# Spreading expert gates with two float32r products instead of one fp32 product, and dealing the routing calls one per chunk

## The reference

```python
def peer(hn, w_q, subkeys, u, v):          # 8 heads, 16 experts per head
    q = (xt @ w_q).reshape(T, H, 2, PEER_QDIM // 2)
    s = jnp.einsum('thcd,cnd->thcn', q, subkeys)
    s1, i1 = lax.top_k(s[:, :, 0], K)
    s2, i2 = lax.top_k(s[:, :, 1], K)
    cand = (s1[..., :, None] + s2[..., None, :]).reshape(T, H, K * K)
    sc, ci = lax.top_k(cand, K)
    e1 = jnp.take_along_axis(i1, ci // K, axis=-1)
    e2 = jnp.take_along_axis(i2, ci % K, axis=-1)
    g = jax.nn.softmax(sc, axis=-1)
    # per token: sum over its 128 chosen experts of gelu(x . u[idx]) * g * v[idx], idx = e1 * 128 + e2
```

## Time and profile before

| | |
|---|---|
| median of 3 runs | 4156.8 us (4156.66 to 4158.11) |
| profiled execution | 4158.48 us, of which span 4157.2 us |
| PE busy / weight loads busy | 3895.5 us (94%) / 3108.8 us (75%) |
| DVE / ACT / POOL busy | 2220.1 (53%) / 1493.4 (36%) / 493.3 us (12%) |
| mean granted TensorE clock | 0.97 of 2.4 GHz |
| chain that ended last | PE 78%, DVE 10%, ACT 5%, DMA 3%, issue 2%, POOL 1% |

### The profile page before, as it was taken

One profiled execution on the slowest core, in us unless ns is written; L12 is line 12 of the kernel. 1 busy time (PEld: TensorE's weight loads), 2 busy tenths in 40 slices (PEclk: granted clock), 3 DMA queues, 4 the chain that ended last, 5 costly groups with the idle time before them and its releaser, 6 DMA issues.

```text
span 4157.2 us, 48351 instructions
## 1 busy us (share of the span) xinstructions
PE 3895.5 (94%) x19998; PEld 3108.8 (75%) x19998; DVE 2220.1 (53%) x3875; ACT 1493.4 (36%) x1876; POOL 493.3 (12%) x748
## 2 busy tenths in 40 slices
PE   6998989999899889988899989999998999999999
PEld 4755778888775568876777878878876788888887
DVE  2275553333557454455554355778873666654444
ACT  3245532122334633234554432435443322222222
POOL 0000000000000000000001000457655111100000
PEclk8999989999999999998999999999999999999999
DMA  5400113323120022231214233355455566543332
GB/s 191 150 34 1 61 41 122 122 102 122 61 76 8 21 71 91 102 128 49 77 41 138 74 116 121 133 162 164 161 172 180 185 186 191 182 149 112 114 127 83
DMA packets 109836, 459.81 MB, mean 111 GB/s; under 512 B 9216, under 2 KB 43120, under 8 KB 68912
## 3 DMA queue, kind: packets, MB, share of 16 engines
q1 hardware_dynamic: 82048, 354.96, 24.5%
q0 software_dynamic: 27568, 101.74, 8.2%
HBM read 389.04 MB, written 67.63 MB: 110 GB/s over the span
## 4 chain that ended last, share of the span: by engine, by line
PE 78%; DVE 10%; ACT 5%; DMA 3%; issue 2%; POOL 1%; SPq 0%; DVEq 0%; ACTq 0%; POOLq 0%
PE ps L566 21%; PE ps L567 21%; PE ps L568 21%; PE ps L2533 1%; PE ps L1176 1%; DMA gdram<-GST 1%; DVE ACC L1377 1%; DVE WL L451 1%; PE ps L480 1%; PE ps L645 1%; POOL Y L2669 1%; DVE MX L1350 1%; PE ps L1255 1%; ACT WH L440 1%; PE ps L2080 1%
## 5 line engine op out<-in xcount | busy, mean ns | idle before, releaser
L566 PE MATMUL ps<-HH,WH 128*128 128x512 f32 x2760 | 1060.0, 384 | 49.6 <-DVE HL L848 20.7
L567 PE MATMUL ps<-HL,WH 128*128 128x512 f32 x2760 | 1046.6, 379 | 0.0
L568 PE MATMUL ps<-HH,WL 128*128 128x512 f32 x2760 | 1042.7, 378 | 0.0
L451 DVE TENSOR_TENSOR WL<-stage,WH 128x2048 fp32r<-128x2048 f32 x248 | 567.4, 2288 | 449.6 <-ACT WH L440 449.6
L440 ACT ACTIVATE WH<-stage 128x2048 fp32r<-128x2048 f32 x248 | 472.7, 1906 | 564.1 <-PE ps L568 522.8
L566 PEld LDWEIGHTS ps<-HH,WH 128*128 128x128 f32 x2760 | 525.8, 191 | 160.2 <-issue 47.2
L568 PEld LDWEIGHTS ps<-HH,WL 128*128 128x128 f32 x2760 | 524.4, 190 | 104.8
L567 PEld LDWEIGHTS ps<-HL,WH 128*128 128x128 f32 x2760 | 525.9, 191 | 99.3 <-issue 1.2
L566 PE MATMUL ps<-AHp,WH 128*128 128x512 f32 x1024 | 404.4, 395 | 7.9 <-ACT Y L2851 7.9
L568 PE MATMUL ps<-AHp,WL 128*128 128x512 f32 x1024 | 404.2, 395 | 0.0
L567 PE MATMUL ps<-ALp,WH 128*128 128x512 f32 x1024 | 404.2, 395 | 0.0
(11 more groups left out here) (410 smaller groups left out, 4890.4 us busy)
## 6 DMA issues: line engine op xcount, KB each, us to landing
stage<-in_w SPq DMA_DIRECT2D x64, 1024.0 KB, 4.9
stage<-in_u SPq DMA_DIRECT2D x64, 1024.0 KB, 4.8
stage<-in_v SPq DMA_DIRECT2D x64, 1024.0 KB, 4.9
stage<-in_w_mod SPq DMA_DIRECT2D x48, 1024.0 KB, 4.9
GR<-gdram POOLq DMA_DIRECT2D x32, 1024.0 KB, 8.1
adram<-GR SPq DMA_DIRECT2D x22, 1024.0 KB, 3.9
AR<-adram POOLq DMA_DIRECT2D x88, 256.0 KB, 3.5
gdram<-GST SPq DMA_DIRECT2D x16, 1024.0 KB, 5.7
```

The lines of the kernel that those rows point to most:

```text
L451: dve.e.tensor_tensor(k.WL[o % 2][:, 0:w], k.stage[n % 2][:, 0:w], k.WH[o % 2][:, 0:w].bitcast(F32), ALU.subtract).then_inc(*dve.done("sla ...
L566: pe.e.matmul(o, wh[:, kk, cs], L.hh[:, kk, z], start=first, stop=False)
L567: pe.e.matmul(o, wh[:, kk, cs], L.hl[:, kk, z], start=False, stop=False)
L568: mm = pe.e.matmul(o, wl[:, kk, cs], L.hh[:, kk, z], start=False, stop=last)
```

## The change

1. The one-hot row with the gate is no longer one fp32 row. ACT copies the gates rounded to float32r (`GH`), DVE takes the remainder from PSUM (`GL`, piece "gates_lo", once per tile). The one-hot matrices become float32r.
2. DVE makes the one-hot rows of 8 tokens in one tensor_tensor of 128x1024 (`hot1`), and the rows times the remainder in a second one ("gated_lo"), where it had 8 tensor_scalar of 128x128. The rows times the rounded gate are made by ACT in place, 8 activations of 128x128 with a scale operand ("gated_hi"), one call after DVE's.
3. PE runs two float32r products per token with the same stationary operand, 16 in a batch, where it ran one fp32 product, 8 in a batch.
4. `route_order` deals the 23 choose pieces of a tile out over 14 calls for the first tile and over the 17 spread calls for the others, and one call follows each chunk: 14 + 4 x 17 = 82 calls for 84 chunks, so none is left over.
5. The waits for the route and the last stores move from before group 21 to its third chunk, just ahead of the weighing of group 0.
6. During the first product with `v`, ACT and DVE weigh group 1 at chunks 3 to 7 instead of 0 to 4 (`weighed_at`).

```diff
 def route_order():
-    phases = [[("choose", 0, 23)]] + [[("spread", t, 17), ("choose", t + 1, 23)] for t in range(3)] + [[("spread", 3, 17)]]
-    for phase in phases:
-        for i in range(max(n for _, _, n in phase)):
-            yield [(kind, tt, i) for kind, tt, n in phase if i < n]
+    for t in range(-1, 4):
+        calls = 14 if t < 0 else 17
+        for i in range(calls):
+            pieces = [("spread", t, i)] if t >= 0 else []
+            yield pieces + [("choose", t + 1, j) for j in range(23 * i // calls, 23 * (i + 1) // calls) if t < 3]
...
 # tensor_route
-                pe.wait_ge("hot1", (tt, b))
+                pe.wait_ge("gated_hi", (tt, b))
                 pe.wait_ge("hot2", (tt, b))
                 for t in range(8):
-                    mm = pe.e.matmul(p[:, 128 * t:128 * t + 128], oh[:, 1, t, :], oh[:, 0, t, :], start=True, stop=True)
+                    pe.e.matmul(p[:, 128 * t:128 * t + 128], oh[2][:, t, :], oh[0][:, t, :], start=True, stop=False)
+                    mm = pe.e.matmul(p[:, 128 * t:128 * t + 128], oh[2][:, t, :], oh[1][:, t, :], start=False, stop=True)
...
 # scalar_route
+        if kind == "spread" and i >= 1:
+            hi = k.OH.of((tt, i - 1))[0]
+            act.wait_ge("gated_lo", (tt, i - 1))
+            for t in range(8):
+                tok = 128 * tt + 8 * (i - 1) + t
+                op = act.e.activation(hi[:, t, :], hi[:, t, :].bitcast(F32), ACT.Copy, scale=k.GH[:, tok:tok + 1])
+            op.then_inc(*act.done("gated_hi", (tt, i - 1)))
...
 # vector_route
-            for t in range(8):
-                tok = 128 * tt + 8 * i + t
-                op = dve.e.tensor_scalar(oh[:, 0, t, :], k.IO[:, :], k.E1[:, tok:tok + 1], k.GG[:, tok:tok + 1],
-                                         ALU.is_equal, ALU.mult)
+            dve.e.tensor_tensor(oh[0], every_expert(k), every_token(k.E1[:, toks]), ALU.is_equal).then_inc(
+                *dve.done("hot1", (tt, i)))
+            dve.wait_ge("hot1", (tt, i))
+            dve.e.tensor_tensor(oh[1], oh[0].bitcast(F32), every_token(k.GL[:, toks]), ALU.mult).then_inc(
+                *dve.done("gated_lo", (tt, i)))
...
 # vector_early (scalar_early the same)
-            for _ in range(route_calls(c)):
-                vector_route(k, dve, next(route, []))
-    for pieces in route:
-        vector_route(k, dve, pieces)
+            vector_route(k, dve, next(route, []))
     dve.mark("route")
-    dve.wait_end("route", "pe", "act", "pool")
-    dve.wait_ge("gst_a", (3, 3))
-    dve.wait_ge("gst_b", (3, 3))
     for c in vector_linear(k, dve, u_linear(k, NPRE - 1)):
         if c == 2:
+            dve.wait_end("route", "pe", "act", "pool")
+            dve.wait_ge("gst_a", (3, 3))
+            dve.wait_ge("gst_b", (3, 3))
             for m in range(5):
                 vector_spilled(k, dve, 0, m)
...
+def weighed_at(g, c):
+    return c - 3 if g == 0 else c
...
             if g + 1 < NPRE:
-                vector_spilled(k, dve, g + 1, c)
+                vector_spilled(k, dve, g + 1, weighed_at(g, c))
```

More of the change, by code:

```diff
@@ L2775, in sync_early @@
                 sp.e.dma_start(io["adram"][g], k.GA.of(g).rearrange("p c t -> p (c t)")).then_inc(*sp.landed("aw", g))
-            for _ in range(route_calls(c)):
-                sync_route(k, sp, io, next(route, []))
-        if g == NPRE - 2:
-            for pieces in route:
-                sync_route(k, sp, io, pieces)
+            sync_route(k, sp, io, next(route, []))
 def p_linear(k, g):
```

56 lines of the change are left out of this document (30 added, 26 removed).

## The result

| | before | after |
|---|---|---|
| median | 4156.7 us | 4178.3 us |
| ratio | | 1.0054 (95% interval 1.0042 to 1.0066) |
| profiled execution / its span | 4158.5 / 4157.2 us | 4177.4 / 4176.1 us |
| first u matmul to first v matmul | 2530.04 to 3202.63, 672.6 us | 2526.81 to 3221.25, 694.4 us |
| POOL / ACT / DVE busy | 493 / 1493 / 2220 us | 620 / 1640 / 2227 us |

The change makes the kernel 21.5 us slower, where 4152 us was forecast. All of it is in the stretch of the route: 21.8 us more there; the profiled execution is only 18.9 longer, because this one came to the stretch 3.2 us earlier. Lines have moved: L566 to L568 are now L569 to L571, the spread product L2533 is L2546 and L2547, POOL's one-hot row L2669 is L2695, DVE's L2587 is the pair L2610 and L2614, ACT's new products are L2576, its copy L2563 is L2584.

The account below looks back on a forecast made before the run. PE was taken as the bound, losing 61.1 us (51.1 in the route, 10.0 at v). 4158.5 - 61.1 + 56.1 of new stops = 4153.5, and 4152 us as median; range 4138 to 4240.

Parts of the forecast that it names:

- Part 1: Spread batches on PE: 16 float32r products last 1.71 us as before, set by weight loads; worth 0.
- rival B: PE's spread products: 128-column float32r costs what fp32 does per column, batch 3.41 us; 4235 us, chance 0.25.
- rival D: PE's weight load is shorter than its pace shows (81 ns), saving 26 us on PE; 4146 us, chance 0.05.
- Part 2: Helpers per call: DVE unchanged, ACT 2.4 us more, POOL from 4.7 to some 6 us, held up by DVE's pair.
- The bookkeeping: Five queues followed call by call through the route; gave the new stops, and 46.5 us for the old order's 51.1.
- rival C: Helpers become the bound, by ACT's products at 0.39 us each or a longer DVE pair; 4170 us, chance 0.15.
- Part 3: New stops in the route: first tile 9.3, three spread tiles 37.1, last tile 5.1, plus 4.6; 56.1 us.
- Part 4: End of route and first product with v: the moved waits leave neither the 25.6 nor the 10.0 us.
- the 25.6: Loss from the bare calls to the first v matmul in the kernel before, in us; was to go.
- the 10.0: Loss in the first product with v in the kernel before, in us; was to go with later weighing.
- my own case: Whole kernel: batches stay 1.71 us and old stops give way to new ones; 4152 us, 4139 to 4167, chance 0.55.
- the 4.6 of shortfall: Route: us added to the new stops because the same count gave 46.5 for the old order, the trace 51.1.

Follow-up runs that it names:

- experiment 6: Kernel after with POOL making 1 of 8 one-hot rows and ACT 1 of 8 products of a batch; 4146.0 us, ratio 0.9980.
- experiment 1: Kernel before with only the new deal of calls, moved waits and later weighing of group 1, old products kept; 4148.4 us, ratio 0.9975.
- experiment 4: Kernel after with DVE's plain rows as 8 one-input instructions and the rows times the remainder left out but for one tiny instruction; 4167.7 us, ratio 1.0024.
- experiment 5: Kernel after with ACT making only 1 of the 8 products of a batch; 4172.0 us, ratio 1.0039.
- experiment 7: Kernel after with 11 thrown-away PE products ahead of the waits for batches 13 and 15 of the three tiles; 4180.9 us, ratio 1.0065.
- experiment 9: Kernel after with group 1 weighed at chunks 0 to 4 again; 4179.0 us, ratio 1.0060.
- experiment 11: Kernel before with new deal by DVE's time, moved waits, odd groups' gates in own memory, group 1 weighed at chunks 0 to 4; 4133.5 us, ratio 0.9954.

## Why the prediction was wrong

**What bounds the kernel, and the sizes of the stretch: right.** The loss of before, 61.1 us, and the new one, 82.6, differ by what the two medians differ by. Small slips change nothing: POOL ended 4.4 us of stops in the kernel before besides the 19.5 named, by its rows in the other buffer; the parts of the 51.1 add up to 50.4; and the first tile's wait is 7.5 by its own terms (1.5 + 78.8 - 72.8), not 7.0.

**Part 1, the products on PE: right.** A batch of 16 records from its first start to the next chunk's:

```profile
2728.18 0.22 PE L2546 MATMUL ps<-OH 128*128 128x128 f32 x1
...
2729.91 0.45 PE L569 MATMUL ps<-HH,WH 128*128 128x512 f32 x1
```

1.73 us, against the 1.71 forecast. The upper bound of rival B, 3.41 us, and its 4235 us fall with it, and so does rival D's 1.30. With the helpers cut in experiment 6, nothing is left that PE would have to answer for. By the Trainium skill (TensorE: Matmul & The Clock Gate, Back-to-back issue gap) the batch would have lasted an estimated 1.30 us; the trace disagrees, 0.108 us for each load and product.

**Part 2, the helpers: the mechanism right, POOL's size wrong. This is the first step that failed.** POOL does stand under DVE's pair, and the sign named for it, over 0.8 us for one row, is there (0.83 and 1.01). DVE's pair in the stretch (mean ns):

```profile
L2610 DVE TENSOR_TENSOR OH<-IO,TA 128x1024 fp32r<-128x1024 f32 x29 | 36.3, 1252 | 21.8 <-PE ps L2547 21.8
...
L2614 DVE TENSOR_TENSOR OHL<-OHY,TD 128x1024 fp32r<-128x1024 f32 x28 | 35.3, 1262 | 1.0
```

It lasts 1.25 and 1.26 us (1.22 forecast), and ACT's 8 products 2.44 (2.4 forecast). For POOL I wrote that it goes from 4.7 to some 6 us per call. It goes to 7.2, and starts from 5.3: the 4.7 was the undisturbed 8 x 0.593, while DVE's L451 and its picking already held POOL up in the kernel before (308.7 us for 469 rows between 2640 and 3142 us, 5.3 for 8; 5.8 with the new deal). To that the new pair adds 1.4 us per batch (7.2 less the 5.8 of experiment 1), 0.7 for each of its instructions instead of the 0.6 taken. 7.3 us is all that a call has, so from here POOL was no longer a helper with room but a bound: the three tiles are 20.0 us longer than with the old products, and up to 15.3 of them are the standstill by experiment 4. The bookkeeping knew of POOL that it gets the gaps between DVE's two-input instructions, but not how few of these there are: batch 13, not 14, is the first that waits. The Trainium skill (SBUF — State Buffer, Who interferes with whom) speaks of a lock that either side may hold. The traces show POOL stand under DVE, while DVE's pair is longer by 0.03 to 0.04 us in the mean, by 0.33 at most; the other direction was part of rival C and is not borne out.

**Part 3, the new deal: right for the first tile (9.3 against 8.5), too small for the others.** In part 2 I said of ACT's 9.14 us behind a store that it "is caught up before PE needs the copy". That is true of the copy, and it is the second step that failed: ACT's new products stand behind that copy, and PE needs them in the next call. This is 6.1 us in the last tile by experiment 5, and with POOL's share there 11.7 by experiment 6. The bookkeeping also had 1.5 us of slow clock per tile where the trace has 6; the half of it behind batch 13 costs nothing, because POOL sets when batch 15 starts, and the other half is open (experiment 7). The sign that I named for being wrong, stops in the middle of the tiles, is what stands there: most of the 8.4 us, and 3.6 in the last tile.

**Part 4, the moved waits: the 25.6 right, the 10.0 wrong.** No stop is left between the last batch and the first v matmul but the slow restart of 2.1 us. But the first product with v loses 10.1 us as before. I had said that it costs 0 to 4 us if `GR` lands 17 or more after the start of v. It lands 19.6 after (3221.25 to 3240.89), and what was left out is the weighing behind it: 13.5 us more until its last part is ready (3254.4), when PE has work for 22.4 us. 19.6 + 13.5 - 22.4 is 10.7 us, wherever the weighing is put: experiment 9 shows the place is worth nothing, experiment 11 that an early landing takes nearly the whole of such a wait away (10.8 us there), of which some 8 reach the time.

**The rivals.** The case that came true is rival C in kind, the helpers as the bound, and like it slower than before; it was given 4170 us and a chance of 0.15, by way of ACT at 0.39 or DVE. It came by way of POOL, whose price I had put in my own case with room to spare. That 4178.3 us lies in the stated 4138 to 4240 is luck: the range was drawn up to there for rival B, which is refuted, and my own case ended at 4167. The sum errs by 26.5 us (82.6 for 56.1): 15.0 in the three tiles, 6.8 in the last, 10.1 at v, less 0.8 in the first and the 4.6 of shortfall. That the deal with the moved waits is a gain was right (forecast about 5 us, measured 8 to 10 with the old products).

## What to carry to other kernels

When a one-input instruction on DVE is replaced by a two-input one of the same length, cost it on POOL: add up what POOL takes per round as it is measured beside DVE's real work, not undisturbed, and compare it with the round. Look too at what it will stand next to: a block of two-input instructions without a pause holds POOL up for its whole length. When an engine gets a product that another waits for, look at what it will be queued behind, here a copy that waits for a store (6.1 us in the last tile); a wait that cost nothing because only a copy hung on it then reaches the critical engine. And a wait that is moved later is gone only if what stands behind it, the weighing, still fits before the data is used.

## What the runs showed of the hardware

- A row of 128x128 on POOL, 0.59 us by itself, took up to 3.68 us and 0.9 in the mean beside DVE's two-input instructions of 1024 and 2048 columns; eight took 11.90 us. One row stood for two of DVE's instructions where they ran without a pause between them (3.67 us over 2.29 and 1.22; 4.59 over twice 2.28 in experiment 4). Those of DVE were hardly held up (1.25 to 1.26 us in the mean against 1.22, at most 1.55).
- float32r products with 128 moving columns and a weight load each start every 0.108 us.
- After a stop of 4 to 5 us PE's next batch ran at a granted clock of 0.50, 3.40 us instead of 1.7. Behind batch 13 that cost this kernel nothing, as POOL was later still; behind batch 15 it is open.
- A load of 64 KB by POOL's queue took 9.7 us from issue to use where one of 1 MB took 11.6 in the same place.
